# One block behind the time mixing, heads computed two ahead of their softmax, and another vector order in the time mixing

## The reference, cut to what matters

```
layer 0: RWKV-7 time mixing (32 heads of 64), then a SwiGLU feed-forward (2048 -> 5632 -> 2048)
layer 1: sparse attention, then a SwiGLU feed-forward
         proj = h @ w_in               -> q, c_kv, q_idx, k_idx, w_idx
         score = sum_h w_idx[h] * relu(q_idx[h] . k_idx)      64 best keys for each query
         logits[h] = (q[h] @ w_uk[h]) . c_kv * scale          other keys barred
         o[h] = softmax(logits[h]) @ c_kv @ w_uv[h]           16 heads of 128
out = rmsnorm(x) * final_norm
```

## Time and profile before

| | us |
|---|---|
| three runs | 3051.05, 3055.96, 3055.96; median 3055.96 |
| the profiled execution | 3054.8 |
| its span | 3053.2 |
| PE busy | 2716.9 (89%) |
| DVE busy | 2014.7 (66%) |
| ACT busy | 1325.3 (43%) |

### The profile page before, as it was taken

How to read it: one execution, slowest core, us unless ns; L and a number is a source line. 1 busy time by engine, 2 the same in 40 slices (tenths; PEclk the granted TensorE clock), 3 DMA queues, 4 the chain that set the end, 5 groups by cost and what they waited for, 6 DMA issues and landing times. The chain is left out here.

```text
span 3053.2 us, 55646 instructions
## 1 busy us (share of the span) xinstructions
PE 2716.9 (89%) x20605; PEld 2370.2 (78%) x20605; DVE 2014.7 (66%) x2613; ACT 1325.3 (43%) x1999; POOL 44.5 (1%) x88
## 2 busy tenths in 40 slices
PE   1299995788889899999999979967889999999998
PEld 0288874778887788888888868857778888888886
DVE  6678830777767777777777786633667765565565
ACT  1255533344434555444444453333445544444444
POOL 1000002000000000000000000000000000000000
PEclk6599997898899999999999989979999999999998
DMA  7679835333327688878788778621557866666653
GB/s 299 247 241 312 293 125 196 122 130 119 125 78 248 212 277 281 290 260 283 259 284 285 238 239 265 213 84 58 175 179 266 281 206 187 189 188 188 187 166 109
DMA packets 472654, 639.97 MB, mean 210 GB/s; under 512 B 21909, under 2 KB 427834, under 8 KB 451770
## 3 DMA queue, kind: packets, MB, share of 16 engines
q1 hardware_dynamic: 468666, 625.31, 61.7%
q0 software_dynamic: 3840, 12.59, 1.1%
HBM read 623.14 MB, written 14.68 MB: 209 GB/s over the span
## 5 line engine op out<-in xcount | busy, mean ns | idle before, releaser
L781 PE MATMUL ps<-act,whi 128*128 128x512 f32 x3808 | 1351.3, 399 | 41.0 <-DVE act L142 18.1
L769 DVE TENSOR_TENSOR wlo<-raw,whi 128x1024 fp32r<-128x1024 f32 (+1 forms) x768 | 901.4, 1192 | 498.8 <-ACT whi L764 497.0
L782 PE MATMUL ps<-act,wlo 128*128 128x256 f32 x3808 | 1073.6, 282 | 0.0
L764 ACT ACTIVATE whi<-raw 128x1024 fp32r<-128x1024 f32 (+1 forms) x768 | 774.3, 1030 | 654.7 <-PE ps L782 650.5
L781 PEld LDWEIGHTS ps<-act,whi 128*128 128x128 f32 x3808 | 723.5, 190 | 216.1 <-DVE wlo L769 27.7
L781 PE MATMUL ps<-hid,whi 128*128 128x512 f32 x2176 | 774.4, 398 | 13.0 <-DVE wlo L769 12.7
L782 PEld LDWEIGHTS ps<-act,wlo 128*128 128x128 f32 x3808 | 728.2, 191 | 0.0
L782 PE MATMUL ps<-hid,wlo 128*128 128x256 f32 x2176 | 615.4, 283 | 0.0
L781 PEld LDWEIGHTS ps<-hid,whi 128*128 128x128 f32 x2176 | 412.3, 189 | 114.0 <-DVE wlo L769 15.6
L782 PEld LDWEIGHTS ps<-hid,wlo 128*128 128x128 f32 x2176 | 411.7, 189 | 0.0
L814 DVE SCALAR_TENSOR_TENSOR ada_acc<-ada_ring,sc,ada_acc 128x2048 f32<-128x2048 f32 x128 | 300.3, 2346 | 0.3
(11 more groups left out here) (274 smaller groups left out, 2392.6 us busy)
## 6 DMA issues: line engine op xcount, KB each, us to landing
raw<-in_f_w SPq DMA_DIRECT2D x480, 512.0 KB, 4.5
ada_ring<-in_ada_w SPq DMA_DIRECT2D x172, 1024.0 KB, 7.4
raw<-in_a_w_rkv SPq DMA_DIRECT2D x96, 512.0 KB, 5.3
raw<-in_b_w_in SPq DMA_DIRECT2D x56, 512.0 KB, 4.5
raw<-in_f_w SPq DMA_DIRECT2D x64, 384.0 KB, 4.1
first_ring<-in_ada_w SPq DMA_DIRECT2D x20, 1024.0 KB, 5.5
raw<-in_a_w_o SPq DMA_DIRECT2D x32, 512.0 KB, 4.8
raw<-in_b_w_o SPq DMA_DIRECT2D x32, 512.0 KB, 6.0
```

What stands on the lines that cost most here:

```text
L764: self.nc.scalar.activation(self.whi[:, u % SPL, 0:n], self.raw[:, u, 0:n], ACT.Copy).then_inc(self.s("hi_ready"), 1)
L769: self.nc.vector.tensor_tensor(self.wlo[:, u % SPL, 0:n], self.raw[:, u, 0:n], self.whi[:, u % SPL, 0:n].bitcast(F32), SUB).then_inc(self. ...
L781: self.nc.tensor.matmul(o, hi[:, kk, c0:c1], src[:, k].rearrange("p a t -> p (a t)"), start=k == 0, stop=False)
L782: last = self.nc.tensor.matmul(o[:, T:2 * T], lo[:, kk, c0:c1], src[:, k, 0, :], start=False, stop=k == ktotal - 1)
```

## The change

Four parts.

*One block.* `index_key`, `index`, `heads` and `final` become classes with one method for each engine, and `build` gives all of them, with the phases ahead and behind, to one `together`. A GpSimd instruction raises a semaphore `cleared` at the block's start, for which `IndexKey` waits. At the end of the `w_in` phase DVE waits for its last two additions and raises nine semaphores that were raised at the head of `index`, and one more.

*The attention.* ACT loads the table set that holds logarithm and exponential ahead of the norms, as `rwkv` does; the square of the index key comes first of the five. The first pair of heads is turned and multiplied on PE behind the score products, without waiting for the key selection. In the loop, PE turns `uk` and multiplies the keys of pair i+1 between the logits of pair i and its turned probabilities, and the values of pair i+1 behind the outputs of pair i. The copy of `kh` goes from DVE to ACT. The last pair is written out.

*The time mixing.* DVE's order in N and C is another (below); `remainder` comes one stage later; the first four rows of pair 0 are added behind its stage M.

*The end.* `nt` has four buffers in place of two, and DVE writes further ahead.

```diff
@@ rwkv, vector @@
-                def stage_M(i):
+                def stage_M(i, late=True):
...
                         tt("P1", b["W"][:], bc(self.ident64), b["XE"][:, :, 0], SUB)
+                    if late:
+                        remainder(i - 2)
@@ stage_N @@
                     rest_of_M3(i)
                     if prep:
                         prep_a(i + 1)
-                    adas(i, 4, 5)
+                    adas(i, 4)
+                    keys(i)
                     if post:
                         centred(i - 1)
-                    for j in range(2):
-                        if prep:
+                    if prep:
+                        for j in range(2):
                             prep_b(i + 1, j)
-                        adas(i, 6 + j)
+                    adas(i, 5)
+                    grow(i, "P2", 1, ADD, "P1")
+                    adas(i, 6, 7)
+                    grow(i, "P3", 1, ADD, "P2")
                     adas(i, 8)
-                    keys(i)
-                    adas(i, 9)
-                    grow(i, "P2", 1, ADD, "P1")
-                    adas(i, 10, 11)
-                    grow(i, "P3", 1, ADD, "P2")
+                    grow(i, "P4", 3, ADD, "P3")
                     if post:
                         normed(i - 1)
-                    adas(i, 12, 13)
-                    grow(i, "P4", 3, ADD, "P3")
-                    if post:
                         gated_in(i - 1, 1 - q)
-                    adas(i, 14)
+                    adas(i, 9, 10, 11, 12)
                     grow(i, "W32", 1, SUB, "P4")
                     if prep:
                         prep_c(i + 1, 1 - q)
-                    adas(i, 15)
+                    adas(i, 13, 14, 15)
                     grow(i, "W64", 3, SUB, "W32")
@@ stage_C, behind the copy of U in chunk c @@
-                        if c == 2:
-                            if post:
-                                gated(i - 1)
-                            if prep:
-                                adas(i + 1, 0)
-                        if c == 3:
-                            if prep:
-                                adas(i + 1, 1, 2, 3)
-                            if post:
-                                remainder(i - 1)
-
-                adas(0, 0, 1, 2, 3)
+                        if prep:
+                            adas(i + 1, c)
+                        if c == 2 and post:
+                            gated(i - 1)
...
-                stage_M(0)
+                stage_M(0, False)
+                adas(0, 0, 1, 2, 3)
@@ class ToProj @@
+    def dve_end(self, dve):
+        p = self.p
+        for g in range(2):
+            dve.wait_ge(p.s(f"group_taken{g}"), p.cgs_of_proj)
+        dve.wait_ge(p.s("cleared"), 1)
+        p.arm(dve, HEADS_ARMED)
+        dve.sem_inc(p.s("proj_done"), 1)
@@ class Attention, scalar @@
+        nc.scalar.preload_act_table_set("natural_log_exp_and_others")
+        for c in (4, 0, 1, 2, 3):
...
+        def body(i, more):
+            if more:
+                queries(i + 1)
+                turned(i + 1)
...
+                last.then_inc(s("exps"), 1)
+            if more:
+                keys(i + 1)
...
+                nc.scalar.activation(p.hid_hi[:, bass.ds(i * 2 + j, 1), :], ps[:, 4 * j + 1:4 * j + 2, 0:T], ACT.Copy).then_inc(s("o_hi"), 1)
+            if more:
+                values(i + 1)
@@ class Attention, tensor @@
+        def body(i, more):
...
+                self.at(pe, "kh", i, j)
+                self.at(pe, "qc", i, j)
+                self.past(pe, "barred_logits", i)
...
+            if more:
+                turn(i + 1)
+                keys(i + 1)
...
+                last.then_inc(s("pturned"), 1)
+            for j in range(2):
...
+                if more:
+                    self.at(pe, "kh", i + 1, j)
...
+            if more:
+                values(i + 1)
+        pe.wait_ge(s("relu"), len(self.jobs))
+        pe.wait_ge(s("ckvt"), 2)
+        pe.wait_ge(s("wq"), 2)
+        turn(0)
+        keys(0)
+        values(0)
+        with pe.Fori(0, self.n - 1) as i:
+            body(i, True)
+        body(self.n - 1, False)
@@ class Final, vector @@
+        for k in range(KT):
+            if k >= 4:
+                dve.wait_ge(s("out_turned"), k - 3)
+            nc.vector.scalar_tensor_tensor(p.nt[:, k % 4, :], p.x[:, k, :], p.pv[:, PV_FN + k:PV_FN + k + 1],
+                                           p.rstd[:], MUL, MUL).then_inc(s("out_normed"), 1)
+            if k >= 3 and k % 2:
+                take(k - 2)
@@ build @@
+        phases.append(IndexKey(self, b_w_o))
+        self.cgs_of_proj = self.cgs + 1
+        heads = Attention(self)
+        phases.append(heads)
+        phases.append(Linear(self, b_w_o, 4, self.ffn_first(1), hid, None, AddGated(self, 8, True), [(0, 3, 170)], ready=heads))
+        phases += self.ffn(1, [[(0, 8, 176)]] + [()] * 5, None)
+        phases.append(Final(self))
         self.together(*phases)
-        self.index_key(b_w_o)
...
-        self.index()
-        self.heads()
...
-        self.together(*phases)
...
-        self.final()
```

More of the change, by code:

```diff
@@ L81, in dve_start @@
     def dve_start(self, dve):
+        pass
+    def dve_end(self, dve):
         pass
@@ L533, in vector @@
                 body(n - 1, True)
+        evac.dve_end(dve)
     def tensor(self, pe):
@@ L568, in pool, with __init__, sync, scalar @@
         self.evac.pool(pool)
+class IndexKey:
+    has_pool = True
+    def __init__(self, prog, following):
+        self.p, self.following = prog, following
+        self.s0, self.p0 = prog.split_units, prog.pairs
+        prog.split_units += 8
+        prog.pairs += 1
+        self.n = 2 * 136
+    def sync(self, sp):
+        p = self.p
+        sp.wait_ge(p.s("cleared"), 1)
+        for u in range(RAW):
+            sp.wait_ge(p.s("unit_split"), self.s0 + u + 1)
+            p.load_unit(sp, u, self.following["source"](0, u))
+    def scalar(self, act):
+        p = self.p
+        act.wait_ge(p.s("cleared"), 1)
+        for u in range(RAW):
+            p.split_hi(act, 0, u, self.s0, self.p0, self.n)
+        act.wait_ge(p.s("unit_used"), self.s0 + 8)
+        p.nc.scalar.activation(p.small_beside_proj[:, 0], p.ps[:, 4:6, T:2 * T], ACT.Copy).then_inc(p.s("key_small"), 1)
+    def vector(self, dve):
+        p = self.p
+        dve.wait_ge(p.s("cleared"), 1)
+        for u in range(RAW):
+            p.split_lo(dve, 0, u, self.s0, self.n)
+        dve.wait_ge(p.s("key_small"), 1)
+        p.nc.vector.tensor_tensor(p.kiw[:], p.ps[:, 4:6, 0:T], p.small_beside_proj[:, 0], ADD).then_inc(p.s("kiw"), 1)
+    def tensor(self, pe):
+        p = self.p
+        pe.wait_ge(p.s("cleared"), 1)
+        for u in range(RAW):
+            pe.wait_ge(p.s("unit_split"), self.s0 + u + 1)
+            p.multiply(u, 2, 2 * u, KT, 136, ((0, P), (8, 136)), p.act, (4, 5)).then_inc(p.s("unit_used"), 1)
+    def pool(self, pool):
+        pool.sem_inc(self.p.s("cleared"), 1)
@@ new lines, with __init__, scalar, vector @@
+class Final:
+    has_pool = False
+    def __init__(self, prog):
+        self.p, self.n0, self.x0 = prog, prog.norms, prog.gateds
+    def scalar(self, act):
+        p = self.p
+        p.rstd_from_sums(act, self.n0)
+        for k in range(0, KT, 2):
+            act.wait_ge(p.s("out_turned"), k + 1)
+            p.nc.scalar.activation(p.fin[:, :, k * P:(k + 1) * P], p.ps[:, k % 4, 0:T].rearrange("p (a n) -> p a n", a=2),
+                                   ACT.Copy).then_inc(p.s("out_even"), 1)
+    def vector(self, dve):
+        p, nc, s = self.p, self.p.nc, self.p.s
+        dve.wait_ge(s("x_added"), self.x0)
+        dve.wait_ge(s("rstd"), self.n0 + 1)
+        def take(k):
+            dve.wait_ge(s("out_turned"), k + 1)
+            nc.vector.tensor_copy(p.fin[:, :, k * P:(k + 1) * P],
+                                  p.ps[:, k % 4, 0:T].rearrange("p (a n) -> p a n", a=2)).then_inc(s("out_odd"), 1)
+        for k in range(KT):
[5 more added lines that the diff above has]
+                take(k - 2)
+        take(KT - 1)
+    def tensor(self, pe):
+        p, nc, s = self.p, self.p.nc, self.p.s
+        p.sum_squares(pe, self.n0)
+        for k in range(KT):
+            pe.wait_ge(s("out_normed"), k + 1)
+            if k >= 4:
+                pe.wait_ge(s("out_even") if k % 2 == 0 else s("out_odd"), (k - 4) // 2 + 1)
+            for a in range(2):
+                last = nc.tensor.transpose(p.ps[:, k % 4, a * P:(a + 1) * P], p.nt[:, k % 4, a * P:(a + 1) * P], p.ident[:])
+            last.then_inc(s("out_turned"), 1)
+    def sync(self, sp):
+        p, s = self.p, self.p.s
+        for q in range(4):
+            sp.wait_ge(s("out_even"), 2 * q + 2)
+            sp.wait_ge(s("out_odd"), 2 * q + 2)
+            at = slice(q * 512, (q + 1) * 512)
+            sp.dma_start(p.out[0].rearrange("(a p) d -> p a d", p=P)[:, :, at], p.fin[:, :, at]).then_inc(s("out_stored"), 16)
+        sp.wait_ge(s("out_stored"), 64)
@@ L1627, in _ @@
```

(3 more changed lines are left out.)

466 lines of the change are left out of this document (212 added, 254 removed).

## The result

| | before | after |
|---|---|---|
| median of the runs beside each other | 3053.51 us (4 runs) | 2973.72 us (4 runs) |
| ratio, 95% interval | | 0.9744, 0.9716 to 0.9772 |
| the profiled execution | 3054.8, span 3053.2 | 2972.63, span 2970.8 |
| PE busy | 2716.9 (89%) | 2692.2 (91%) |

The forecast was 2983 (2969 to 3001); the change gave 9 us more than that.

What follows compares the result with a forecast made beforehand. PE bounds the `w_in` phases; in time mixing and attention the chain from engine to engine bounds. Gains of 21 + 0.5 + 2.9 + 15.8 + 26.9 + 5.4 = 72.5 us off 3054.8 gave 2983 us for the median, range 2969 to 3001.

Steps and rivals of the forecast that it cites:

- behind `w_in`: Border behind `w_in`: ACT splits at once without the border; gain 0.5 us, between 0 and 1.1.
- time mixing: Time mixing: DVE's new order shortens PE's waits and the slow products behind them; gain 21 us, bounds 4 and 30.
- norms: Norms of the attention: four table loads go and one comes, mostly hidden; gain 2.9 us, bounds 1.5 and 5.
- first pair: First pair of heads: PE works on it beside the key selection; gain 15.8 us, bounds 10 and 16.2.
- seven periods: Heads' loop: the new order cuts a period from 16.54 to 12.7 us; gain 26.9 us over seven.
- Pair 0: Start of the time mixing: 5.4 us from moving four row additions, 3.6 from early `BF`; gain 9.0 us.
- Small ones: Next weights' split 1.0, second feed-forward norm's table load 1.3, the end 3.1; together 5.4 us, bounds 2 and 7.
- (a): Rival, time mixing: it gives only its start; 2999 us, chance 0.17.
- (b): Rival, heads: the granted clock stays as before or ACT's list becomes the chain; period 14.7, 2997 us, chance 0.11.
- (c): Rival, first pair of heads: it ends up behind the selection, 10 us lost; 2993 us, chance 0.05.
- (d): Rival, heads' loop: it pays 5.4 us at each of six jumps back; 3015 us, chance 0.04.
- (e): Rival, merged block: all 33 jumps back stall at 5.4 us each, making it slower; 3161 us, chance 0.03.

Runs made afterwards that it cites:

- kernel 4: Changed kernel with the four row additions of pair 0 ahead of `prep_a` again, as before; 2985.9 us, ratio 0.9766 to the kernel before.
- Kernel 3: Changed kernel with DVE's old order in stage N of the time mixing alone; 3001.5 us, ratio 0.9823 to the kernel before.
- kernel 9: Changed kernel with DVE's nine semaphore raises moved from the end of `w_in` to behind its index-key weight splits; 2981.5 us, ratio 0.9759 to the kernel before.
- the repetition: The changed kernel timed once more, unchanged, as the yardstick; 2978.1 us, ratio 0.9735 to the kernel before.
- kernel 7: Changed kernel with the heads' old order: turn, values, keys of the next pair behind the outputs; 3014.8 us, ratio 0.9865 to the kernel before.
- kernel 10: Changed kernel with PE's loop over pairs 1 to 6 of the time mixing written out; 2969.2 us, ratio 0.9718 to the kernel before.
- kernels 6 and 7: Changed kernel with the next pair's work behind the outputs, as turn, keys, values (3017.0 us, 0.9871) or turn, values, keys (3014.8 us, 0.9865).
- kernel 5: Changed kernel with PE waiting for the bar on the keys before the first pair of heads; 2992.7 us, ratio 0.9779 to the kernel before.

## Why the prediction was right, step by step

The forecast's direction, its order of size and the place of each gain held, save the 0.5 behind `w_in`. In the two profiles, stretch by stretch, and on means over all traces with the same code:

| step | forecast | the two profiles | means |
|---|---|---|---|
| time mixing (A) | 21 | 24.3 | 22.7 |
| behind `w_in`, norms, first pair (B, C) | 0.5 + 2.9 + 15.8 = 19.2 | 18.5 | C alone 18.8 |
| seven periods (D) | 26.9 | 29.2 | 28.9 |
| next weights, second norm (in E) | 2.3 | 5.7 | 1.0 |
| end (F) | 3.1 | 3.7 | 3.8 |
| the start of the time mixing | 0 | 0.9 | |

- **Time mixing.** The sum was right, its split was not. Pair 0: 9.0 forecast, 7.8 measured (from `kk` to the head of pair 1, 61.6 to 53.8); by kernel 4 the rows give 4.6 of it at that point, and 2 at the end of the stage, where 5.4 were forecast. The 3.6 for `BF` was a slip (6.0 less 2.6 is 3.4), and the wait itself went from 3.92 to 2.04. From DVE's `XE` of one pair to that of the next, pairs 1, 2, 4, 6 gained 4.2, 3.1, 2.4 and 4.3 against 3.4 each, and 3 and 5 gained 0.2 and -0.1 against -0.4. Kernel 3 shows that stage N's order gives 20.5 of the 22.7, where the forecast without its start had 15.6. That the sum came out so close is in part luck.
- **Behind `w_in`: mis-sized, with the wrong sign.** Forecast a gain of 0.5; PE's wait there rose from 2.74 to 3.00, a loss of 0.26, because DVE's raises stand ahead of the split and PE waits for DVE's half, not for ACT's (kernel 9). The step took ACT's 1.15 as the bound of the gain and left DVE's raises without a price.
- **Norms: mis-sized in that profile.** From `kiw` to the first `relu` it was 12.2 before, 10.6 after (1.6), and 9.3 to 10.2 in the nine other traces that have the load there, so 2.4 on the mean (12.2 less 9.8) against 2.9. "Most of it beside the sum of the index key" was wrong: the load began 0.02 before that sum and outlasted it by 0.6.
- **First pair.** 16.0 behind the bar, 15.8 forecast, but for another reason in part. The forecast priced PE at a low clock and had the first softmax 0.5 behind the bar for it; PE began at 1987.50, ran keys and values in 3.72 and 3.73 at the full clock and was done with the logits before the bar. And 4.3 of the gain are loads that the border had kept back, which the forecast didn't see.
- **Periods.** 12.48 against 12.7, granted clock 1.00, waits 0.51 and 0.25 against 0.5 and 0.5. The first period took only 11.46 in that profile (12.27 in the repetition), so the mean was 12.33 against 16.51, a gain of 29 and not 26.9. PE's clock of before went with its gaps: with the old order (kernel 7) it is 0.89 again.
- **Small ones.** From the last remainder of the attention to PE's first product with the next weights it is 0.93 less (2.83 to 1.90), 1.0 forecast; both loads in the second feed-forward's norm are gone, one forecast. The other 3.4 us of E lie in code that is the same, and the means don't show them.
- **Rivals.** (a) fell by kernel 3, (b) and (c) by the trace. (d) and (e): the heads' loop has no idle time of PE above 0.56, and B and E, where most of the 33 jumps lie, did not grow. That the stalls in pairs 3 and 5 are the jump back is now shown by kernel 10; that the length of the body makes the difference to the other loops is argued only.

By the means the steps sum to some 75 us; the timings say 70 to 87 (interval of the ratio). What lies between can't be told from chance in B and E.

## What to carry to other kernels

When one engine's work for the next item can run beside another's for this one, price what the gaps cost twice: the idle time, and the slower clock of the products behind them; the same work in one row behind the item (kernels 6 and 7) was slower in the heads than what was there. A border between blocks holds back loads as well as engines, so read from which transfer the first product behind it waits. And before an edit of a few microseconds is judged, let a few executions of unchanged code show how far a stretch moves by itself.

## What the runs showed of the hardware that was not expected

- *A jump back of PE in the loop of the time mixing costs 5.1 to 6.2 us*, at the head of pairs 3 and 5 in each of the twelve traces with the loop; written out, both are gone. The body holds some 1800 matrix products (5477 for six pairs, two pairs in a body). The loops of the heads (80 products in a turn) and of the large products show none.
- *DVE's semaphore raises cost 0.09 us each*: with nine of them moved, PE's wait for the split behind them fell from 3.00 to 2.16, and DVE's own idle time ahead of the split from 1.05 to 0.21.
- *The granted clock behind a short wait differs between executions of the same code*: 0.80, 0.89 or 1.00 over the index key, between whose ends lie 2.65 us (17.08 and 14.43).
- *PE's busy time in a stretch that it bounds is not fixed.* From the time mixing to the end of `w_in`, with the same 5800 products, it was 1024.39 us in the profile after and 11 us more in kernel 5, at the same granted clock to two digits; DVE and ACT are within 0.3. Busy time by stretch in kernel 5:

```profile
897.60:1963.00 1065.40, 1035.48 (x5799) 898.49 (x5800) 794.89 (x762) 477.91 (x561) 0.00 (x0) 0.97 0.77 259
```

What makes an execution slower there stays open.
